# Differential attention units: both softmaxes' rows are transposed and multiplied with the values, and the difference is taken of the results

## What is computed

```
def diff_mixer(q, k, v, lam_vecs, sub_g, lam_init, cos, sin):
    ...
    lam = jnp.exp(jnp.sum(lv[0] * lv[1])) - jnp.exp(jnp.sum(lv[2] * lv[3])) + lam_init
    ...
        s = jnp.einsum('bqhcd,bkhcd->bhcqk', qb, k) * scale
        p = masked_softmax(s, kpos[None, :] <= tq[:, None])
        a = p[:, :, 0] - lam * p[:, :, 1]
        return jnp.einsum('bhqk,bkhd->bqhd', a.astype(v.dtype), v)
```

## Time and profile before

| | us |
|---|---|
| median of three runs | 2106.82 |
| lowest and highest | 2106.23, 2110.12 |
| profiled execution, whole | 2106.95 |
| its span | 2105.1 |
| TensorE busy | 1959.5 |
| VectorE busy | 655.4 |
| ScalarE busy | 311.6 |
| differential units, layer 0 | about 107 to 134 |
| differential units, layer 1 | about 535 to 561 |

### The profile page before, as it was taken

One profiled execution on the slowest core, in us unless ns is written; L12 is line 12 of the kernel. 1 busy time (PEld: TensorE's weight loads), 2 busy tenths in 40 slices (PEclk: granted clock), 3 DMA queues, 4 the chain that ended last, 5 costly groups with the idle time before them and its releaser, 6 DMA issues.

```text
span 2105.1 us, 21965 instructions
## 1 busy us (share of the span) xinstructions
PE 1959.5 (93%) x8546; PEld 1079.7 (51%) x8546; DVE 655.4 (31%) x1270; ACT 311.6 (15%) x741; POOL 84.4 (4%) x127
## 2 busy tenths in 40 slices
PE   8988999999889999899999999999899999899886
PEld 4555677755557676774444434443785333233221
DVE  2473334224643333474311111111424211111113
ACT  2442000014420000203211101110101100000000
POOL 3102000001020000200000000000000000000000
PEclk9998999999999999999999999999999999999998
DMA  9216787642158776527699999999536799999995
GB/s 310 76 61 187 243 275 265 228 150 74 61 163 284 260 272 241 169 58 307 258 383 427 428 427 428 428 427 417 203 139 260 319 422 429 428 428 427 428 426 244
DMA packets 158898, 603.07 MB, mean 286 GB/s; under 512 B 16776, under 2 KB 73016, under 8 KB 128080
## 3 DMA queue, kind: packets, MB, share of 16 engines
q1 hardware_dynamic: 153728, 591.43, 72.0%
q0 software_dynamic: 4880, 10.22, 1.8%
q10 hardware_dynamic: 192, 0.05, 0.0%
HBM read 597.67 MB, written 1.10 MB: 284 GB/s over the span
## 4 chain that ended last, share of the span: by engine, by line
PE 72%; DMA 18%; DVE 5%; issue 2%; ACT 1%; DVEq 1%; ACTq 1%; SPq 0%
PE ps L1987 15%; PE ps L790 15%; DMA ring<-in_e_w_gate 9%; PE ps L796 7%; DMA ring<-in_e_w_up 7%; PE ps L522 7%; PE ps L2005 5%; PE ps L1821 4%; PE ps L1786 3%; PE ps L1834 3%; PE ps L1915 3%; PE ps L1930 2%; PE ps L618 2%; DMA ring<-in_e_w_down 1%; PE ps L602 1%
## 5 line engine op out<-in xcount | busy, mean ns | idle before, releaser
L790 PE MATMUL ps<-hT,ring 128*128 128x256 f32 x1408 | 315.1, 386 | 1.5 <-DVE hT L284 1.5
L790 PEld LDWEIGHTS ps<-hT,ring 128*128 128x128 f32 x1408 | 278.8, 199 | 33.9 <-issue 4.0
L1987 PE MATMUL ps<-ring,hT 128*64 128x512 f32 (+1 forms) x1024 | 234.1, 610 | 27.5 <-DMA ring<-in_e_w_up 14.1
L2005 PE MATMUL ps<-ring,qkT 128*64 128x512 f32 (+1 forms) x1024 | 226.6, 594 | 6.4 <-ACT qkT L2202 4.5
L1987 PE MATMUL ps<-ring,late 128*64 128x512 f32 (+1 forms) x960 | 213.3, 597 | 20.3 <-DMA ring<-in_e_w_up 11.1
L522 PE MATMUL ps<-ring,hT 128*128 128x512 f32 (+1 forms) x384 | 170.8, 597 | 2.3 <-DMA ring<-in_w_in 1.5
L1987 PEld LDWEIGHTS ps<-ring,hT 128*64 128x64 f32 (+1 forms) x1024 | 73.0, 126 | 184.5 <-issue 184.5
L796 PE MATMUL ps<-ring,late 128*128 128x512 f32 x352 | 154.7, 593 | 0.0
L1987 PEld LDWEIGHTS ps<-ring,late 128*64 128x64 f32 (+1 forms) x960 | 66.8, 124 | 160.8 <-issue 160.8
L2005 PEld LDWEIGHTS ps<-ring,qkT 128*64 128x64 f32 (+1 forms) x1024 | 68.7, 123 | 145.5 <-issue 145.4
L1270 DVE SCALAR_TENSOR_TENSOR qkT<-ring,cc,qkT 128x512 f32<-128x512 f32 x168 | 125.9, 750 | 10.0
(11 more groups left out here) (381 smaller groups left out, 1681.1 us busy)
## 6 DMA issues: line engine op xcount, KB each, us to landing
ring<-in_e_w_down SPq DMA_DIRECT2D x64, 2048.0 KB, 16.2
ring<-in_e_w_up SPq DMA_DIRECT2D x64, 2048.0 KB, 17.3
ring<-in_e_w_gate SPq DMA_DIRECT2D x60, 2048.0 KB, 17.2
ring<-in_ada_w SPq DMA_DIRECT2D x24, 2048.0 KB, 10.4
ring<-in_w_gate SPq DMA_DIRECT2D x22, 1024.0 KB, 7.7
ring<-in_w_up SPq DMA_DIRECT2D x22, 1024.0 KB, 10.0
ring<-in_w_down SPq DMA_DIRECT2D x22, 1024.0 KB, 12.2
ring<-in_w_in SPq DMA_DIRECT2D x8, 2048.0 KB, 14.2
```

What stands on the lines that cost most here:

```text
L790: last = mm(m.ps[:, c, at:at + SEQ], w[:, j, c, :], m.hT[:, j, :], start=(j == 0), stop=(j == KC - 1))
L1987: last = mm(dst, xg[:, j, at + x * n_tok:at + (x + 1) * n_tok], w(x, j), start=(j == 0), stop=(j == KC - 1))
L2005: lasts[x] = mm(dst, m.hidT[:, j, rows + x * n_tok:rows + (x + 1) * n_tok], half_of(w(x, j), n), start=(j == 0), stop=(j == 3))
```

## The change

For the differential units VectorE no longer makes rows of differences. It only makes the reciprocals and scales those of the second softmaxes by minus lambda. The four sets of exponentials, not normalised, all go through TensorE's transposes (four instead of two for each tile of keys), ScalarE's copy (four sets wide) and the products with the values (four, where the two softmaxes of a head use the same values). unit_out then multiplies the four results by the four reciprocals into a temporary (the tile ucT, which the units win and cmp use in the same way) and adds the two halves of each head into O.

```diff
@@ unit_values
-    return [(pair, Z_BV + HD * (2 * pair + g)) for pair in range(2)]
+    return [(pair + 2 * part, Z_BV + HD * (2 * pair + g)) for pair in range(2) for part in range(2)]
@@ transposed
-            for h in range(2 if kind == "diff" else 4):
+            for h in range(4):
@@ transposed_out
-            elif kind == "diff":
-                last = a(m.pt[:, 0:2, 0:t + 1, :], pt[:, 0:2, 0:t + 1, :], ACT.Copy)
@@ probabilities
-                ts(odd, odd, m.lam[:, 5:6], None, ALU.mult)
-                for h in range(2):
-                    ts(pr[:, h, :], pr[:, h, :], rs[:, 2 * h:2 * h + 1], None, ALU.mult)
-                dve.drain()
-                for h in range(2):
-                    last = stt(pr[:, h, :], pr[:, 2 + h, :], rs[:, 2 * h + 1:2 * h + 2], pr[:, h, :], ALU.mult, ALU.add)
+                last = ts(odd, odd, m.lam[:, 5:6], None, ALU.mult)
@@ unit_out
-                last = v.tensor_copy(m.O[:, t, cols:cols + GW].rearrange("p (s g d) -> p s g d", s=2, g=2)[:, :, g, :],
-                                     src[:, 0:128].rearrange("p (s d) -> p s d", s=2))
+                tmp = m.ucT[:, 0, :].rearrange("p (h d) -> p h d", d=HD)
+                dve.drain()
+                tt(tmp, src4, scale, ALU.mult)
+                dve.drain()
+                parts = m.ucT[:, 0, :].rearrange("p (s c d) -> p s c d", s=2, c=2)
+                last = tt(m.O[:, t, cols:cols + GW].rearrange("p (s g d) -> p s g d", s=2, g=2)[:, :, g, :], parts[:, :, 0, :], parts[:, :, 1, :], ALU.add)
```

## The result

The changed kernel takes 2110.88 us (median of 14 runs, 2109.1 to 2112.88) beside 2107.21 us for the kernel before (14 runs, 2105.61 to 2110.12). The ratio is 1.0016, with a 95% interval of 1.0008 to 1.0023: 3.7 us slower, between 1.7 and 4.8. The prediction was 2107.1 us in a range of 2104.2 to 2111.2.

A forecast was written before the change was run, and what follows sets the result against it. TensorE, busy 93% of the span and 72% of the chain, bounds the kernel. Added work, less shorter waits and a recovered clock, leaves 0.13 + 0.16 = +0.29 us: 2106.82 + 0.29 = 2107.1 us, range 2104.2 to 2111.2.

The forecast's parts named there:

- TensorE's added work: Extra transposes and value products: 0.66 us in units 4 and 6, 1.33 in 5 and 7, 3.98 us a layer.
- Unit 7's scores: On TensorE after unit 5's added work: start 1.28 us later, at 119.21 instead of 117.93.
- VectorE's result: Reaches TensorE 0.94 us after VectorE and products are ready: drain 0.09, scaling 0.50, addition 0.29, TensorE's start 0.06.
- unit 5's transposes: Behind the first stall: start 0.05 us earlier, 113.02 instead of 113.07, after a pause near 0.3 us.
- Unit 7's transposes: Behind the second stall: unit 6's result arrives 0.49 us later, TensorE's pause shrinking to 0.96 and 0.59 us.
- The clock at unit 7 stays high: Behind the second stall, eight transposes and the half projection (3.44 us) run at 2.4 GHz in both layers.
- the first rival: Clock still falls at the second stall: 2110.9 us, about 2109 for one layer; chances 0.10 both, 0.11 one.
- One sign of being right: In the profile after, TensorE's busy time would be up by clearly less than 8 us.
- so I let the shift arrive whole: Behind the attention the shift of 0.13 + 0.16 = +0.29 us was carried unchanged to the whole kernel's time.
- the clock's relief: Full clock at unit 7 brings its products 0.77 and 0.74 us earlier, +0.13 and +0.16 with the added products.
- One more fall behind unit 10 in layer 0: Low clock at unit 10's scores too, adding 1.6 us to both layers low: 2112.5 us, chance 0.03.

The follow-up runs named there:

- second pair of traces: Both kernels run again without edits: changed kernel 2111.51 us, ratio 1.0015; kernel before against itself 1.0000.
- experiment 7: Kernel before with idle transposes in four pauses a layer, plus 32 more ahead of the feed-forward part: 2094.25 us, ratio 0.9932.
- experiment 4: Idle transposes in four pauses of each layer, in both kernels: kernel before 2099.59 us (0.9961), changed kernel 2102.77 us (0.9977).
- rows kept: Changed kernel's TensorE and ScalarE work, but VectorE still makes rows of differences as in the kernel before: 2113.61 us, ratio 1.0024.
- one pause filled: Kernel before with 12 idle transposes in the pause before unit 7's transposes: 2107.56 us beside 2108.55, ratio 0.9997.
- units 5 and 7: Kernel before with the change in units 5 and 7 only, the old way in the other differential units: 2109.09 us, ratio 1.0007.
- units 4 and 6: Kernel before with the change in units 4 and 6 only, the old way in the other differential units: 2108.71 us, ratio 1.0009.
- changed, unit 10's pause filled: Changed kernel with 14 idle transposes in the pause before unit 10's scores, no other pause filled: 2110.34 us, ratio 1.0014.

## Why the prediction was off

The time lies inside the range, but the forecast of no change to speak of, 2107.1 us, was 3.8 us short, and the measured loss is real.

- TensorE's added work, 0.66 and 1.33 us a unit: right. Unit 7's scores came 12.07 us after unit 4's transposes (before 10.79), +1.28 as worked out.
- VectorE's result, 0.94 us: right. The addition took 0.29 us, and unit 5's transposes start 0.95 us after unit 4's products end (113.60 to 114.55); they are 0.05 us early, as forecast, behind a pause of 0.31.
- Unit 7's transposes: +0.49 forecast. Layer 0 has 19.55 us from unit 4's (before 19.18), +0.37, layer 1 19.30 (before 18.80), +0.50. Behind layer 0's are two errors that partly cancel: VectorE is ready 0.37 us earlier than forecast (line 1116 ends at 127.03), and then waits 0.34 us for nothing that the profile shows, where 0.09 was allowed.
- The clock at unit 7 stays high: right, in both traces and both layers. The half projection fell to 3.60 us, and the first rival (low clock in the same place) did not happen. That its 2110.9 us equals the result is chance.
- One sign of being right failed: TensorE's busy time was to grow by clearly less than 8 us and grew by 9.1 (5.8 in the second pair of traces).
- The failed step is "so I let the shift arrive whole". I booked the clock's relief, 1.7 us a layer, as saved for the whole kernel. It was saved in the unit, but in these traces the low clock of the attention stayed at 26 to 28 us in all. Where fillers take the clock out of the comparison, the work costs 3.5 us, and that is what the whole kernel shows (3.7, and 3.0 in the second timing): the clock paid for next to none of it. One more fall behind unit 10 in layer 0, priced at 1.6 us, stood only as an addition to the first rival; it belonged to the forecast itself.
- The differences by stretch in the first traces are: +1.53 us ahead of unit 4 in layer 0 (not repeated: the second trace of before has 109.01 there, the changed kernel 108.74), +0.01 and +0.16 in the stretch, +0.39 and +1.17 behind it, -0.74 between the two layers' attention, +1.50 in layer 1's units 0 to 3. Together +4.0; the other 1.2 us of the span come after. The code behind unit 13's transposes of layer 1 is the same in all kernels but that of experiment 7, and took 1504.4 to 1510.1 us in the eleven traces. One or two traces cannot part this further.

The other variants bear the failed step out. Differences from the kernel before in us: of the two stretches from those of experiment 4's filled kernel (24.02 + 23.67), which is the work with the clock taken out; of the attention from unit 0's transposes to unit 13's in both layers (194.35 in the first trace of before, 194.80 in the second); of the whole by the medians, each good to about 2 us:

| | stretches at full clock | attention in its trace | time |
|---|---|---|---|
| changed kernel | +3.5 | +3.2 | +3.7 |
| rows kept | +5.3 | +1.1 | +5.1 |
| one pause filled | 0.0 | -0.7 | -1.0 |
| units 5 and 7 | -0.2 | -2.0 | +1.5 |
| units 4 and 6 | +2.4 | -1.9 | +1.1 |
| changed, unit 10's pause filled | +3.6 | -3.8 | +2.9 |

The time goes with the first column within 1.7 us. It does not go with the second: rows kept, units 4 and 6, and the last one have 8.7, 8.6 and 5.6 us of delay by the clock in the attention of their traces, the kernel before 12.9 and 13.4, and none of the three is faster. So it is not so that the attention's low clock always stays the same and only moves; where such relief goes, when it does not arrive, is not shown.

What stays open is what decides which pause is followed by the low clock. 2.21 and 1.84 us were (kernel before, unit 7), 2.06 and 1.75 were not (units 4 and 6 alone; rows kept), and 1.95 was in one layer and not in the other. In the second trace of before the clock fell in unit 4 with no pause right ahead. So it is also open why filling one pause gains so little and filling four gains 8.0 us of the 9.5 that they save in place (stretches and the parts behind them).

## What to carry to other kernels

Where an engine is busy for 93% of the span and stands for 72% of the chain, added work on it costs its full length wherever the time is not truly idle: here 2.2 of 3.98 us a layer fell into such time or were made good by the shorter wait, and 1.8 remained. A clock that recovers behind one stall was no saving here while other such stalls followed: 0.6 to 1.0 us of 3.4 arrived. With four of them filled 8.0 us arrived, so the sum should carry no credit for a single one. Idle work in TensorE's waits, cut so that it ends before the wait does, cost nothing in place and was worth far more here (13 us) than the shortening of a wait.

## What the runs showed of the hardware that I had not expected

TensorE's clock fell to 1.2 GHz behind many pauses of about 2 us amid otherwise full work, and cost 1.6 to 1.7 us at unit 7 and at unit 10, and 2.9 us behind the 2.16 us pause of unit 12 in layer 0. It fell once with no pause right ahead (unit 4 in the second trace of before). Filling four such pauses in each layer with 52 useless transposes gave 8.0 us (0.39%), and 32 more ahead of the feed-forward part another 5.3 us, though TensorE's instructions grew.
